# A two-layer decoder step: the VectorE order of the cached-page loop, its buffers, and two TensorE products rearranged

## The chip, the cores and the metric

The kernel runs on one core of a Trainium2 chip. TensorE (PE) multiplies matrices out of on-chip memory (SBUF) into eight accumulation banks (PSUM), VectorE (DVE) and ScalarE (ACT) read and write both, GpSimd (POOL) works on SBUF, and SyncE (SP) issues the transfers. Each engine runs its own instruction list in order and waits on semaphores. The metric is the device time of one execution in microseconds.

## What is computed

One inference step of a decoder of two layers, on a prompt of 1024 tokens and on eight samples of eight new tokens each. The three mixers of a layer are a latent attention (MLA, 8 heads), a gated linear attention and an attention over a memory. The change touches the sampled part of MLA alone: each sample attends to 32 cached pages of 128 positions, found through a page table. The core of the reference for one page:

```python
c_blk = cache_ckv[layer, phys]              # (8, 128, 256) latent
kpe_blk = cache_kpe[layer, phys]            # (8, 128, 32)  positional key, not yet rotated
k = _mla_keys(c_blk, kpe_blk, pos, w_uk, g_k)   # k_nope = c @ w_uk; rmsnorm over (k_nope, kpe); rotate the last 32
sc = einsum('bthd,bphd->bhtp', q, k) * MLA_SCALE
m_new = maximum(m, s.max(-1)); alpha = exp(m - m_new); p = exp(s - m_new[..., None])
l_new = l * alpha + p.sum(-1)
acc_new = acc * alpha[..., None] + einsum('bhtp,bpr->bhtr', p, c_blk)
```

## The kernel before

Each layer has three stages: nine tiles of projections (eight of the prompt, one of the sample), the **page loop**, and the output projection. The page loop is what changes. It takes the 8 x 32 pages of a layer in 32 groups of G = 8 pages, four groups for each sample, so 64 groups in all; `k` counts groups in a layer, `j` pages in a group, and `n0` or `np_` groups or pages over both layers. On the groups with low numbers ride small steps of the sample's other work (`sample_step(k, j)`), such as the eight products over the new tokens (`NEW_VALUES`, page steps (1,6), (1,7), (2,0) to (2,4) and (3,0)), each of which TensorE may begin when VectorE has copied out the one before.

One group, engine by engine:

- **SP** copies raw pages to a scratch tensor in DRAM in an arrangement that is cheap to transpose (`copy_pages`, L403; most are copied during the prompt, the last 28 of a layer one in each group), loads that arrangement for half a group (`load_quarters`, L420), the positional keys page by page (`load_kpe`, L412), and the pages as they are (`load_pages`, L428, which waits until the values of two groups before have been used). At the head of each group's transfers it waits until all copies issued so far have landed (`gathered`).
- **VectorE** turns the quarters into latents by position with a stream transpose (`turn_quarters`, L1017, four in a group, two pages each; `pcT_ready` tells TensorE). A ring of six such pairs lies in `region`, `xT` and `W`.
- **TensorE** multiplies each page with `w_uk` (`keys`, L1911, two products of 128x512 float32, each of which is two records in the trace), into bank 2 or 3 by turns.
- **ScalarE** squares the product (L874) into one of two buffers `sqb`, **VectorE** sums the squares for each head (L1396) into `pst`. ScalarE waits for the sum of the page two before, TensorE for the square of the page two before (`pkn_sq`).
- **GpSimd** rotates the positional keys of the eight pages (L652 to L655) and squares the unrotated ones (L656). TensorE turns the rotated ones (`rotT`, L1968) after page 1.
- After page 7 VectorE and ScalarE form the factor of each key from the sums (L1401 to L1407), while TensorE makes the scores (`scores_of`, L1927 for the latent part, L1929 for the rotary part) and then the values of the group before (`values`, L1941). VectorE scales the scores into `psb` (L1413) and takes maxima over the pages (L1415).
- The maxima of group k - 1 are finished in group k: TensorE turns them after page 3 (`maxima_T`, L1946), VectorE reduces them and lays the running maximum on a diagonal `dg` (L1424 to L1429), TensorE spreads it over all partitions with a product against ones after page 5 (`maxima_over`, L1950), VectorE subtracts (L1432) and ScalarE takes the exponential (L886).

Everything is in one hand-written order on each engine: a late instruction of VectorE holds back all of its later ones. In the rows, an instruction's names are those of the whole allocation: `w_in` holds `sqb`, `pst`, `dg`, `pm` and from group 20 on the loaded pages; `region` holds `psb`, `rotT` and the rings; `U` holds the queries.

## Time and profile before

| | |
|---|---|
| median of three runs | 2888.56 us (2888.01 to 2888.64) |
| profiled execution | 2889.7 us, of which the span from first to last instruction is 2887.9 us |
| PE busy | 2804.5 us, 97% |
| DVE busy | 1892.6 us, 66% |
| ACT busy | 880.6 us, 30% |
| POOL busy | 332.9 us, 12% |
| mean granted TensorE clock | 0.994 |

The page loops run from 664.8 to 1341.2 us and from 2078.7 to about 2757 us of the span, nearly half of it. The matmul records' ends are modelled: a record lasts about 0.16 us longer than until the next one starts, so a gap on TensorE is longer by that than the idle time that the profile prints, and gaps below 0.16 us are not printed at all.

### The profile page before, as it was taken

How to read it: one execution, taken by the hardware profiler on the slowest of the kernel's cores; microseconds unless marked ns; L12 is line 12 of the kernel's file. 1: busy time of each engine (PE TensorE's matmuls, PEld its weight loads, DVE VectorE, ACT ScalarE, POOL GpSimd, SP SyncE). 2: the span in 40 equal slices, each digit the busy share in tenths (PEclk: the TensorE clock that was granted, in tenths of full speed). 3: DMA queues.
4: the chain of work that ended last, by engine and by line, in shares of the span. 5: the costliest groups of instructions: out<-in, count | busy, mean ns of one | idle time of the engine just before them, and what ended most of it. 6: DMA issues, size and time to landing. Idle time of an engine off the chain costs nothing.

```text
span 2887.9 us, 56735 instructions
## 1 busy us (share of the span) xinstructions
PE 2804.5 (97%) x19061; PEld 1666.9 (58%) x19061; DVE 1892.6 (66%) x3801; ACT 880.6 (30%) x1903; POOL 332.9 (12%) x467
## 2 busy tenths in 40 slices
PE   8999999998999999999999999999989999999999
PEld 5666677664445554545466667767544555554553
DVE  3666665557787778776245666655678787877742
ACT  1333333432323333332023333333223333333300
POOL 1111000002111111110010000000111111111100
PEclk9999999999999999999999999999999999999999
DMA  7222223334334434543532222233443444445432
GB/s 279 73 65 68 70 72 74 72 90 137 107 108 116 124 112 124 151 147 123 212 122 59 65 69 70 71 74 72 135 113 101 115 117 123 116 121 174 116 106 84
DMA packets 528949, 313.85 MB, mean 109 GB/s; under 512 B 360009, under 2 KB 512146, under 8 KB 525586
## 3 DMA queue, kind: packets, MB, share of 16 engines
q1 hardware_dynamic: 526912, 309.41, 37.4%
q8 instruction: 152, 2.49, 0.4%
q14 instruction: 139, 1.14, 0.1%
q10 hardware_dynamic: 1746, 0.81, 0.1%
HBM read 287.63 MB, written 89.60 MB: 131 GB/s over the span
## 4 chain that ended last, share of the span: by engine, by line
PE 56%; DVE 21%; SPq 10%; DMA 6%; issue 4%; ACT 4%; POOL 0%; DVEq 0%; ACTq 0%
PE ps L1505 11%; PE ps L1911 10%; PE ps L1989 8%; DVE w_in L1396 5%; SPq L398 3%; PE ps L1739 3%; PE ps L1499 3%; PE ps L1927 3%; DMA pages_by_quarter<-in_cache_ckv 2%; SPq L428 2%; PE ps L1941 2%; DVE region L1017 2%; SPq L403 2%; PE ps L1511 2%; PE ps L1516 2%
## 5 line engine op out<-in xcount | busy, mean ns | idle before, releaser
L1911 PE MATMUL ps<-w_uk,region 128*128 128x512 f32 x1040 | 474.1, 598 | 2.9 <-ACT w_in L874 1.6
L874 ACT ACTIVATE w_in<-ps 128x512 f32<-128x512 f32 x512 | 305.7, 597 | 497.1 <-PE ps L1911 402.5
L1396 DVE TENSOR_REDUCE w_in<-w_in 128x8 f32<-128x512 f32 x512 | 351.3, 686 | 136.5 <-ACT w_in L874 121.5
L1505 PE MATMUL ps<-w_in,xT 128*128 128x256 f32 (+6 forms) x1360 | 379.1, 432 | 0.6
L1911 PE MATMUL ps<-w_uk,xT 128*128 128x512 f32 x672 | 309.0, 602 | 3.1 <-ACT w_in L874 3.1
L1911 PEld LDWEIGHTS ps<-w_uk,region 128*128 128x128 f32 x1040 | 186.3, 190 | 217.1 <-issue 206.1
L1505 PEld LDWEIGHTS ps<-w_in,xT 128*128 128x128 f32 (+1 forms) x1360 | 246.9, 186 | 111.9 <-issue 69.3
L603 POOL TENSOR_TENSOR rs<-us,mhalf 128x1 f32<-128x1 f32 (+4 forms) x132 | 130.9, 991 | 1351.1 <-DVE us L1033 729.8
L1911 PEld LDWEIGHTS ps<-w_uk,xT 128*128 128x128 f32 x672 | 121.6, 192 | 138.9 <-issue 133.8
L1911 PE MATMUL ps<-w_uk,W 128*128 128x512 f32 x336 | 151.7, 593 | 0.0
L1929 PE MATMUL ps<-U,region 128*64 128x64 f32 x2048 | 149.3, 224 | 0.0
L1739 PE MATMUL ps<-region,W 96*128 96x512 f32 (+3 forms) x384 | 147.5, 497 | 0.1
L1511 PE MATMUL ps<-w_in,xT 128*128 128x256 f32 (+1 forms) x496 | 142.9, 431 | 0.0
L1224 DVE TENSOR_REDUCE st<-ps 128x1 f32<-128x256 f32 (+7 forms) x128 | 97.0, 758 | 68.0 <-PE ps L1740 64.3
L652 POOL TENSOR_TENSOR xt<-region,mkv 128x128 f32<-128x128 f32 x64 | 29.2, 457 | 967.3 <-issue 942.0
L792 ACT ACTIVATE U<-ps,us 128x256 f32<-128x256 f32 (+7 forms) x128 | 94.8, 740 | 121.4 <-DVE us L1225 85.9
L1989 PE MATMUL ps<-region,glw 128*128 128x512 f32 x256 | 113.2, 595 | 0.0
L1989 PE MATMUL ps<-region,xT 128*128 128x512 f32 x256 | 112.3, 594 | 0.0
L1927 PEld LDWEIGHTS ps<-U,region 128*64 128x64 f32 x2080 | 86.0, 142 | 41.7 <-issue 41.7
L1927 PE MATMUL ps<-U,region 128*64 128x64 f32 x2080 | 99.9, 228 | 9.7 <-DVE U L1286 9.7
L1929 PEld LDWEIGHTS ps<-U,region 128*64 128x64 f32 x2048 | 106.2, 140 | 0.0
L1511 PEld LDWEIGHTS ps<-w_in,xT 128*128 128x128 f32 x496 | 89.4, 190 | 28.8
(403 smaller groups left out, 4183.8 us busy)
## 6 DMA issues: line engine op xcount, KB each, us to landing
pages_by_quarter<-in_cache_ckv SPq DMA_DIRECT2D x512, 128.0 KB
region<-pages_by_quarter SPq DMA_DIRECT2D x80, 512.0 KB, 4.0
region<-in_cache_ckv SPq DMA_DIRECT2D x320, 128.0 KB, 2.2
w_in<-pages_by_quarter SPq DMA_DIRECT2D x48, 512.0 KB, 4.0
w_in<-in_cache_ckv SPq DMA_DIRECT2D x192, 128.0 KB, 2.2
w_in<-in_w_in SPq DMA_DIRECT2D x16, 1240.0 KB, 10.5
mix_quarters<-xn SPq DMA_DIRECT2D x16, 512.0 KB, 3.8
region<-in_cache_kpe SPq DMA_DIRECT2D x512, 16.0 KB
```

The source lines that it names most:

```text
L603: pool.tensor_tensor(rs[0:T, c:c + k], us[0:T, c:c + k], mhalf[0:T, 0:k], ALU.pow).then_inc(s.root_ready, 1)
L792: tell(act.activation(pt[:, h % 2, 0:nk], src, ACT.Exp, bias=us[:, 52 + h % 2:53 + h % 2], scale=SCALE, accum_out=st[:, 52 + h:53 + h]), s ...
L874: tell(act.activation(sqb[:, j % 2, :], ps[:, j if k == 0 and j < 2 else 2 + j % 2, :], ACT.Square), s.pkn_sq, np_)
L1224: own(dve.tensor_reduce(st[:, 62 + h % 2:63 + h % 2], src, X, ALU.max))
L1396: tell(dve.tensor_reduce(pst[:, 0, j * H:j * H + H], heads(sqb[:, j % 2, :], H), X, ALU.add), s.pkn_red, np_)
L1505: ins = mm(out, xT[:, k, 0:T], w_in[:, k, c0:c0 + w], start=k == 0, stop=k == KD - 1)
L1511: ins = mm(out, xT[:, k, 0:T], w_in[:, k, c0:c0 + w], start=k == 0, stop=k == KD - 1)
L1739: ins = mm(ps[:, bank + c // 512, 0:w], qT[:, h, :], kT[:, h, c:c + w], start=True, stop=not last)
L1911: ins = mm(ps[:, key_bank(k, j), :], page[:, o_:o_ + P], w_uk[:, c, :], start=c == 0, stop=c == 1)
L1927: ins = mm(so, page[:, o_:o_ + 64], qt[:, c, 64 * b:64 * b + 64], start=c == 0, stop=False)
L1929: ins = mm(so, rotT[:, j // 4, half:half + 64], qrz[:, j % 4, 64 * b:64 * b + 64], start=False, stop=True)
L1989: ins = mm(ps[:, 2 + c, :], m_T[p][:, k, :], w_out[:, k, 512 * c:512 * c + 512], start=k == 0, stop=k == KD - 1)
```

## The change

The computed result is the same. Seven things move:

1. **VectorE order.** The quarters 2 and 3 of a group are turned together ahead of page 0 (before: ahead of pages 1 and 3). Quarter 0 of the next group is turned after page 5 (before: ahead of it), quarter 1 after the statistics have been handed to ScalarE (before: ahead of page 7). The reduction of the maxima moves from behind page 3 to ahead of page 2's sum (`group_max`), the subtraction from behind page 5 to behind page 4 (`less_max`), the sum of the positional squares from page 0 to page 2.
2. **Four square buffers** `sqb` in place of two. ScalarE waits for the sum of the page four before. It takes the exponential behind page 6 (before: 5).
3. **Rotary products in pairs.** In place of two products of 128 rows x 64 columns x 64 for each page (16 in a group, three quarters of whose rows meet zeros), there are eight of 64 rows x 64 columns x 128, each for two pages, after all the latent products. GpSimd writes the rotated keys in the order that this needs; it makes the squares first and rotates in place.
4. **Banks.** The scores of pages 0 to 3 go to bank 0 and those of pages 4 to 7 to bank 1 (before: all to bank 4).
5. **The product that spreads the maxima** is made as two products of 64 output partitions (`halves`).
6. **SP order.** The page copy goes ahead of the second half of the positional keys, the load of `w_out` parts ahead of them all; before, both were last.
7. **Group 1's first quarters** are loaded right behind group 0's pages, ahead of its positional keys and of the 4 MB of memory keys and values.

```diff
-        sqb = scratch[:, 16640:17664].rearrange("p (b n) -> p b n", b=2)
+        sqb = [scratch[:, o_:o_ + 512] for o_ in (16640, 17152, 18648, 19160)]
...
                 load_pages(0, held[0])
+                load_quarters(1, 0)
                 load_kpe(1, 0, G, held[1])
...
-                    load_quarters(k, 0)
+                    if k > 1:
+                        load_quarters(k, 0)
+                    if LATE + 4 <= k < LATE + 4 + NG:
...
                     load_quarters(k, 1)
+                    if copied < DB * PAGES:
+                        copy_pages(copied, copied + 1)
+                        copied += 1
                     if k + 1 < DB * NG:
                         load_kpe(k + 1, G // 2, G, held[k + 1])
                     load_pages(k, held[k])
-                    if copied < DB * PAGES:
-                        copy_pages(copied, copied + 1)
-                        copied += 1
...
-                    own(pool.tensor_tensor(kr, kp, cosp[:, tab, :], ALU.mult))
-                    own(pool.tensor_tensor(kr, kr, rt, ALU.add))
-                    pool.tensor_tensor(rtmp[:, 1, :], kpr[:, q, :], kpr[:, q, :], ALU.mult).then_inc(s.kpe_rot, 1)
+                    own(pool.tensor_tensor(rtmp[:, 1, :], kpr[:, q, :], kpr[:, q, :], ALU.mult))
+                    own(pool.tensor_tensor(kp, kp, cosp[:, tab, :], ALU.mult))
+                    pool.tensor_tensor(krot[:, q, :].rearrange("p (c r n) -> p c r n", c=2, r=2), by_half[0], by_half[1], ALU.add).then_inc(s.kpe_rot, 1)
...
-                        if np_ >= 2:
-
-                            act.wait_ge(s.pkn_red, np_ - 1)
+                        if np_ >= 4:
+
+                            act.wait_ge(s.pkn_red, np_ - 3)
...
-                    if j == 5:
+                    if j == 6:
                         act.wait_ge(s.psub_ready, n0 + 1)
...
-                        if j in (1, 3):
-                            turn_quarters(k, (j + 3) // 2)
-                        if j in (5, 7) and k + 1 < DB * NG:
-                            turn_quarters(k + 1, (j - 5) // 2)
+                        if j == 0:
+                            turn_quarters(k, 2)
+                            turn_quarters(k, 3)
                         sample_step(k, j)
...
+                        if k and j == 2:
+                            group_max(k - 1)
+                        if j == (2 if k else 3):
...
+                        if k and j == 4:
+                            less_max(k - 1)
+                        if j == 5 and k + 1 < DB * NG:
+                            turn_quarters(k + 1, 0)
...
                     tell(ts(pst[:, 1, :], pst[:, 0, :], 1.0 / QK, EPS, ALU.mult, ALU.add), s.pu_ready, n0)
+                    if k + 1 < DB * NG:
+                        turn_quarters(k + 1, 1)
                     dve.wait_ge(s.r_exp, n0 + 1)
...
+                        page, so_ = pcT(k * (G // 2) + j // 2), 64 * (j % 4)
+                        for c in range(2):
                             for half in range(0, P, 64):
...
+                                mm(ps[half:half + 64, j // 4, so_:so_ + 64], page[:, o_:o_ + 64], qt[:, c, 64 * b:64 * b + 64], start=c == 0 and j % 4 == 0, stop=False)
+                    for c in range(2):
+                        for half in range(0, P, 64):
+                            for r in range(2):
+                                w = slice(64 * r, 64 * r + 64)
+                                ins = mm(ps[half:half + 64, r, P * c:P * c + P], rotT[w, c, half:half + 64], qrz[w, 2 * r:2 * r + 2, 64 * b:64 * b + 64], start=False, stop=c == 1)
                     ins.then_inc(s.ps_ps, 1)
...
-                    mm(ps[:, 7, 384:512], ones[:], dg, start=True, stop=True).then_inc(s.pmb_ps, 1)
+                    halves(ps[:, 7, 384:512], ones[:], dg, P, True, True).then_inc(s.pmb_ps, 1)
```

**VectorE, a group with no sample steps, from the first page's sum on, before.** L1396 is a page's sum, L1017 a transpose (of two pages), L1424 to L1429 the maxima of the group before.

```order
L1396 TENSOR_REDUCE w_in<-w_in 128x8 [waits pkn_sq,kk_ready]
L1017 STREAM_TRANSPOSE region<-w_in 128x2x4x64 [waits ps_ps,bulk_in_3,pkn_red]
L1396 TENSOR_REDUCE w_in<-w_in 128x8 [waits pkn_sq,pcT_ready]
L1396 TENSOR_REDUCE w_in<-w_in 128x8 [waits pkn_sq,pkn_red]
L1017 STREAM_TRANSPOSE xT<-w_in 128x2x4x64 [waits ps_ps,bulk_in_3,pkn_red]
L1396 TENSOR_REDUCE w_in<-w_in 128x8 [waits pkn_sq,pcT_ready]
L1424 TENSOR_REDUCE w_in<-ps 128x1 [waits pmT_ps,pkn_red]
L1426 TENSOR_TENSOR w_in<-w_in,m 128x1 [waits dve_step]
L1427 TENSOR_TENSOR w_in<-m,w_in 128x1 [waits dve_step]
L1428 TENSOR_SCALAR m<-w_in 128x1 [waits dve_step]
L1429 TENSOR_SCALAR w_in<-ident,w_in 128x128 [waits dve_step]
```

The same place now; the transpose is L1018, the maxima L1427 to L1432, the sum of the positional squares L1394.

```order
L1018 STREAM_TRANSPOSE region<-w_in 128x2x4x64 [waits ps_ps,bulk_in_3,pacc_ready]
L1018 STREAM_TRANSPOSE xT<-w_in 128x2x4x64 [waits ps_ps,bulk_in_3,pcT_ready]
L1396 TENSOR_REDUCE w_in<-w_in 128x8 [waits pkn_sq,pcT_ready]
L1396 TENSOR_REDUCE w_in<-w_in 128x8 [waits pkn_sq,pkn_red]
L1427 TENSOR_REDUCE w_in<-ps 128x1 [waits pmT_ps,pkn_red]
L1429 TENSOR_TENSOR w_in<-w_in,m 128x1 [waits dve_step]
L1430 TENSOR_TENSOR w_in<-m,w_in 128x1 [waits dve_step]
L1431 TENSOR_SCALAR m<-w_in 128x1 [waits dve_step]
L1432 TENSOR_SCALAR w_in<-ident,w_in 128x128 [waits dve_step]
L1394 TENSOR_REDUCE w_in<-xt 128x8 [waits kpe_rot,pd_ready]
L1396 TENSOR_REDUCE w_in<-w_in 128x8 [waits pkn_sq,kk_ready]
```

Two page sums and the positional sum now stand behind the maxima; the transposes stand first.

**TensorE, from the last product of page 5 to the scores, before.** L1950 spreads the maxima, L1927 and L1929 are the latent and the rotary part of the scores.

```order
L1911 MATMUL ps<-w_uk,region 128x512
L1950 MATMUL ps<-w_in,ones 128x128 [waits pd_ready]
L1911 MATMUL ps<-w_uk,xT 128x512 [waits pkn_sq,pcT_ready]
L1911 MATMUL ps<-w_uk,xT 128x512
L1911 MATMUL ps<-w_uk,xT 128x512 [waits pkn_sq,pcT_ready]
L1911 MATMUL ps<-w_uk,xT 128x512
L1927 MATMUL ps<-U,region 64x64 [waits rotT_evac]
L1927 MATMUL ps<-U,region 64x64 x3
L1929 MATMUL ps<-U,region 64x64 x2
L1927 MATMUL ps<-U,region 64x64 x4
L1929 MATMUL ps<-U,region 64x64 x2
```

The same place now; L1506 is the spread in halves, L1918 the keys, L1932 and L1937 the scores, L1949 the values.

```order
L1918 MATMUL ps<-w_uk,region 128x512
L1506 MATMUL ps<-w_in,ones 64x128 [waits pd_ready]
L1506 MATMUL ps<-w_in,ones 64x128
L1918 MATMUL ps<-w_uk,xT 128x512 [waits pkn_sq,pcT_ready]
L1918 MATMUL ps<-w_uk,xT 128x512
L1918 MATMUL ps<-w_uk,xT 128x512 [waits pkn_sq,pcT_ready]
L1918 MATMUL ps<-w_uk,xT 128x512
L1932 MATMUL ps<-U,region 64x64 [waits rotT_evac]
L1932 MATMUL ps<-U,region 64x64 x23
L1932 MATMUL ps<-U,xT 64x64 x8
L1937 MATMUL ps<-U,region 64x128 x8
L1949 MATMUL ps<-region 64x257 [waits pacc_ready,bulk_in_1,pp_ready]
```

The rotary products are one block of eight between latent products and values.

**SP, at the turn of a group, before.** The copy (L403) and the load of `w_out` are followed at once by the quarters of the next group, which wait for the copy.

```order
L398 ISA x2
L403 ISA
L403 DMA pages_by_quarter<-in_cache_ckv 512x1x64
L522 DMA region<-in_w_out 128x2048
L420 DMA w_in<-pages_by_quarter 128x4x256 [waits pcT_ready,gathered]
L398 ISA x2
L412 ISA
```

Where the copy stands now, between the second quarters and the positional keys:

```order
L420 DMA w_in<-pages_by_quarter 128x4x256 [waits pcT_ready]
L398 ISA x2
L403 ISA
L403 DMA pages_by_quarter<-in_cache_ckv 512x1x64
L398 ISA x2
L412 ISA
L412 DMA region<-in_cache_kpe 128x32
```

Four positional keys and eight pages now stand between a copy and the next wait for it.

## Rows read from the trace of the kernel before

**Rows 1.** The page: engines, busy us, share, instructions.

```profile
PE 2804.5 (97%) x19061; PEld 1666.9 (58%) x19061; DVE 1892.6 (66%) x3801; ACT 880.6 (30%) x1903; POOL 332.9 (12%) x467
```

**Rows 2.** Waits of TensorE: us in total, times, longest.

```profile
PE ps L1950 <- DVE w_in L1429: 24.8, 34, 1.1
PE ps L1927 <- DVE U L1286: 9.7, 2, 4.9
...
PE ps L1911 <- ACT w_in L874: 4.6, 4, 1.6
```

**Rows 3.** Windows: length, busy of the engines, clock, DMA. Groups 20-29, group 21.

```profile
1101.38:1302.87 201.49, 195.15 (x1492) 102.34 (x1490) 157.60 (x285) 65.37 (x132) 30.09 (x50) 1.00 0.48 140
1122.37:1141.54 19.17, 19.17 (x151) 10.31 (x149) 14.58 (x26) 6.08 (x12) 2.99 (x5) 1.00 0.44 124
```

**Rows 4.** Timeline of VectorE in group 24, which starts at 1181.35.

```profile
1192.42 0.29 DVE L1424 TENSOR_REDUCE w_in<-ps 128x1 f32<-128x128 f32 x1
...
1193.33 0.29 DVE L1429 TENSOR_SCALAR w_in<-ident,w_in 128x128 f32<-128x128 f32 x1
...
1195.37 1.11 DVE L1017 STREAM_TRANSPOSE xT<-w_in 128x512 f32<-128x512 f32 x1 [1.03 <-DMA w_in<-pages_by_quarter]
...
1197.23 0.69 DVE L1432 TENSOR_TENSOR region<-region,ps 128x512 f32<-128x512 f32 x1
1199.61 0.69 DVE L1396 TENSOR_REDUCE w_in<-w_in 128x8 f32<-128x512 f32 x1 [1.69 <-ACT w_in L874]
```

**Rows 5.** SyncE: quarters issued in group 24 (timeline), and its longest wait.

```profile
1189.97 0.39 SPq L420 DMA_DIRECT2D w_in<-pages_by_quarter  x1
...
1195.40 0.43 SPq L420 DMA_DIRECT2D w_in<-pages_by_quarter  x1
...
SPq L420 <- DMA pages_by_quarter<-in_cache_ckv: 149.2, 53, 3.9
```

**Rows 6.** Timeline of TensorE in a group that waits for nothing.

```profile
1119.83 0.40 PE L1927 MATMUL ps<-U,W 128*64 128x64 f32 x8
...
1120.06 0.29 PE L1929 MATMUL ps<-U,region 128*64 128x64 f32 x4
...
1120.18 0.40 PE L1927 MATMUL ps<-U,W 128*64 128x64 f32 x8
...
1120.53 1.91 PE L1941 MATMUL ps<-region 128*64 128x257 f32 x16
...
1122.37 3.70 PE L1911 MATMUL ps<-w_uk,region 128*128 128x512 f32 x8
...
1133.11 0.38 PE L1950 MATMUL ps<-w_in,ones 128*128 128x128 f32 x2
...
1133.33 3.60 PE L1911 MATMUL ps<-w_uk,xT 128*128 128x512 f32 x8
...
1136.86 0.45 PE L1927 MATMUL ps<-U,region 128*64 128x64 f32 x8
```

**Rows 7.** Timeline of TensorE: products in two row tiles, in four column tiles.

```profile
1485.04 1.13 PE L1639 MATMUL ps<-mkv,ws 64*128 64x256 f32 x8 [0.19 <-DVE ws L1045]
...
1038.94 1.97 PE L1874 MATMUL ps<-w_in 128*32 128x256 f32 x32
```

**Rows 8.** Group 0: timelines of SyncE, VectorE, TensorE, and a window as in 3.

```profile
674.49 2.86 SPq L420 DMA_DIRECT2D region<-pages_by_quarter  x1
...
685.10 1.07 DVE L1017 STREAM_TRANSPOSE xT<-region 128x512 f32<-128x512 f32 x1 [5.06 <-DMA region<-pages_by_quarter]
...
688.88 0.70 PE L1927 MATMUL ps<-U,region 128*64 128x64 f32 x8 [4.82 <-DVE U L1286]
...
686.90:693.70 6.80, 4.83 (x91) 4.86 (x92) 6.01 (x9) 0.60 (x1) 0.00 (x0) 0.50 0.51 153
```

**Rows 9.** Timeline of TensorE in group 2, which starts at 721.70.

```profile
726.81 0.65 PE L1838 MATMUL ps<-ck,w_in 64*64 64x257 f32 x2 [0.42 <-DVE ws L1314]
...
732.47 0.65 PE L1838 MATMUL ps<-ck,w_in 64*64 64x257 f32 x2 [0.51 <-DVE ws L1314]
```

More of the change, by code:

```diff
@@ L642, in _ @@
                     rt = rtmp[:, 0, :].rearrange("p (j n) -> p j n", j=G)
-                    kr = krot[:, q, :].rearrange("p (j n) -> p j n", j=G)
+                    by_half = [x_.rearrange("p (r c n) -> p c r n", r=2, c=2) for x_ in (kpr[:, q, :], rtmp[:, 0, :])]
                     tab = slice(g * G, g * G + G)
@@ L870, in act_group @@
                         act.wait_ge(s.pkn_ps, np_ + 1)
-                        if np_ >= 2:
-                            act.wait_ge(s.pkn_red, np_ - 1)
-                        tell(act.activation(sqb[:, j % 2, :], ps[:, j if k == 0 and j < 2 else 2 + j % 2, :], ACT.Square), s.pkn_sq, np_)
+                        if np_ >= 4:
+                            act.wait_ge(s.pkn_red, np_ - 3)
+                        tell(act.activation(sqb[j % 4], ps[:, j if k == 0 and j < 2 else 2 + j % 2, :], ACT.Square), s.pkn_sq, np_)
                         if k:
@@ L889, in _ @@
                     act_group(k)
[L890 removed]
+                softmax(DB * NG - 1, 6)
                 act.wait_ge(s.fold_ready, 4 * L + 2)
@@ L1395, in dve_group @@
                         dve.wait_ge(s.pkn_sq, np_ + 1)
-                        tell(dve.tensor_reduce(pst[:, 0, j * H:j * H + H], heads(sqb[:, j % 2, :], H), X, ALU.add), s.pkn_red, np_)
-                        if k:
-                            softmax(k - 1, j)
+                        tell(dve.tensor_reduce(pst[:, 0, j * H:j * H + H], heads(sqb[j % 4], H), X, ALU.add), s.pkn_red, np_)
+                        if k and j == 4:
+                            less_max(k - 1)
+                        if j == 5 and k + 1 < DB * NG:
+                            turn_quarters(k + 1, 0)
+                        if k == DB * NG - 1 and j == G - 2:
+                            turned(0)
                     u3 = pst[:, 0, :].rearrange("p (j h) -> p j h", j=G)
@@ L1434, in gather, with less_max @@
+                def less_max(k):
+                    n0 = L * DB * NG + k
+                    sg = psb[:, k % 2, :].rearrange("p (j n) -> p j n", n=P)
+                    dve.wait_ge(s.pmb_ps, n0 + 1)
+                    tell(tt(sg, sg, over_heads(ps[:, 7, 384:512], P, G // 2, P), ALU.subtract), s.psub_ready, n0)
                 def gather(k):
@@ L1920, in scores_of @@
                     for j in range(G):
[L1921 to L1922 removed]
+                        page, so_ = pcT(k * (G // 2) + j // 2), 64 * (j % 4)
+                        for c in range(2):
                             for half in range(0, P, 64):
[L1924 to L1929 removed]
+                                o_ = (j % 2) * R + c * P + half
+                                mm(ps[half:half + 64, j // 4, so_:so_ + 64], page[:, o_:o_ + 64], qt[:, c, 64 * b:64 * b + 64], start=c == 0 and j % 4 == 0, stop=False)
[4 more added lines that the diff above has]
+                                ins = mm(ps[half:half + 64, r, P * c:P * c + P], rotT[w, c, half:half + 64], qrz[w, 2 * r:2 * r + 2, 64 * b:64 * b + 64], start=False, stop=c == 1)
                     ins.then_inc(s.ps_ps, 1)
```

47 lines of the change are left out of this document (15 added, 32 removed).

## The prediction

> **What bounds the kernel now.** I read the page first, then the waits of TensorE, then windows of whole groups, then the timelines of single groups. The page shows TensorE busy for 97% of the span and VectorE for 66% [rows 1], so time can only come from TensorE's own work or from its gaps, and only in the page loops, since nothing else is touched. The waits put the gaps of the loops at two places: the product that spreads the maxima waits 34 times for VectorE's diagonal, 24.8 us, and the first scores of each layer wait 4.8 us for the queries, 9.7 us; four key products add 4.6 us [rows 2]. A group that waits for nothing takes 19.17 us; groups 20 to 29 take 201.49 us, 9.8 us more than ten such groups [rows 3]. VectorE works 14.6 to 15.8 us of each, so it has room; it is late by its order and by what it waits for.
>
> Why it is late shows in group 24, which starts at 1181.35 and takes 20.85 us. The maxima are reduced at 1192.42 and the diagonal is ready at 1193.6, that is at 12.3; TensorE has done six pages (six times 1.72 us, and 0.33 us of turning) at 10.65. Then VectorE waits 1.03 us for a transfer, its subtraction comes at 1197.23, ScalarE sits in the exponential that needs it, and the page's square behind that exponential keeps VectorE waiting 1.69 us [rows 4]. The lateness is carried into the next group. The transfer is late because SyncE issues the quarters only when the page copy just issued has landed, a wait that sums to 149.2 us over 53 times; in group 24 they go out at 8.6 and 14.05 after the group's start [rows 5].
>
> **Part by part.** T is a group's start.
>
> *VectorE order, buffers, SyncE order (1, 2, 6).* With four square buffers neither ScalarE nor TensorE needs a recent sum, and I lay VectorE's work out with the durations of [rows 4]: a transpose 1.11, a sum or a subtraction 0.69, the maxima 1.20. The statistics of page 7 are in at about T + 15.7, the transpose of quarter 1 fills the time in which ScalarE makes the roots, the scores are scaled and the next maxima taken by T + 19.9, 0.7 into the next group. There: accumulate 1.2, two transposes 3.4, two sums 4.9, then a wait for TensorE's turned maxima, which come after page 3 at 7.4. The diagonal is ready at 8.6, 2.0 us before TensorE asks at 10.65. VectorE has 2.5 us of waiting there, which absorbs lateness instead of passing it on. SyncE no longer waits for a copy it has just issued: pages out by T + 4, quarters at 4.4 and 8.5, needed at 12.4 and at 1.2 of the next group, so some 4 us after issue there are 4 and 8 us to spare. The gain: 24.8 us; each of the 34 gaps is 0.16 us longer than printed, since the last of eight key records is printed beyond its turn (3.60 us for eight that follow each other by 0.43) [rows 6], which adds 5.5; the four key waits with theirs, 5.3; behind a gap the second record of a product starts about 0.10 late, some 40 times, 4; and short gaps ahead of page 4 that fall below what is printed, 3. That makes 43. Ten groups give 9.8 [rows 3], 64 at that rate 63, with the sample steps' own work in it; 43 lies below that. I take 41 and 25 to 43 as bounds.
>
> *First quarters (7).* In group 0 VectorE waits 5.06 us for the quarters of group 1, issued at 674.49 behind 4 MB of other loads; the query copies stand behind that transpose, TensorE waits 4.82 us for them, and then the granted clock is 0.50 of full, 1.2 instead of 2.4 GHz, for 6.8 us with 4.83 us of work in it [rows 8]. Loaded ahead of those, the quarters are there by 675. VectorE would copy the queries by 683.7, TensorE has its last key product out at 683.9. So 9.7 us over both layers go, and half of the 4.83 us that ran at half clock, some 2.1 per layer beyond the printed tails, 4.3. A second stretch of half clock follows in group 1 under products of eight columns; I leave it in. Sum 14.0, bounds 9 and 17.
>
> *Rotary products (3, 4).* A page's scores take 0.35 us, of which the rotary part is the 0.12 from 1120.06 to 1120.18 [rows 6]: 0.93 for a group. Now there are 16 records of 128 columns. 256 columns take 0.216 a wave: two row tiles of L1639 make four waves in its 1.13 us, four column tiles of L1874 eight waves in 1.97 [rows 7]. So 128 columns take 0.109, and four quadrants at once make 4 waves, 0.44. No row has row and column tiles together. Changing between tile shapes costs: eight key records should end at 1133.33 + 8 x 0.429 = 1136.76, the scores start at 1136.86, 0.10 later; 16 values records should end at 1120.53 + 8 x 0.216 = 1122.26, the keys start at 1122.37, 0.11 later, and the first keys then take 3.70 instead of 3.60 [rows 6]. The block adds two changes, each 0.10 and about 0.04 for the first wave's weights: 0.27. Net 0.93 - 0.44 - 0.27 = 0.22, 64 times: 14 gained. Bounds: all four never at once, 8 waves, 14 lost; changes free, 31 gained.
>
> The Trainium skill, page "TensorE: Matmul & The Clock Gate", section "Measured speedup vs the span model", has row and column tiles running together, 16 of them at 10.6 times. By it the 4 waves hold and the sum stays; the other reading is a rival below.
>
> *The spread in halves (5).* Before: 0.22 us from 1133.11 to 1133.33, no change of shape. Now two waves of 128 columns, the same 0.22, and a change in and out in the middle of the keys: 0.10 and 0.04 in, 0.11 out and 0.10 on the first keys [rows 6]. 0.34, 64 times: 22 lost. Bound below: where TensorE still waited, the way in is free, 0.2 each, 13.
>
> The Trainium skill speaks against this part: page "TensorEngine Tiling (Array Packing)", section "Key Properties", says that changing the tiling mode drains TensorE. The 0.10 of the rows agrees. The page gives no price; by a reading with free changes the result would be 22 us better and the rotary part 17.
>
> *New waits.* Two transposes now stand ahead of the sample steps of page 0, and the maxima ahead of those of pages 2 and 3. In group 2, TensorE's products over the new tokens each need VectorE's copy of the last. At page 1 the copy comes at about T + 4.1 where TensorE asks at 1.9; at page 4 it comes behind the maxima, at 14.3 where TensorE asks at 11.5. 5.0 against the 0.9 waited there now [rows 9], 4.1 for each layer, 8; in group 1 ScalarE's square waits for the sample's scores, 1 for each layer. Together 10, bounds 2 and 14. GpSimd's reordering, the banks and the earlier `w_out` cost nothing: keys are rotated by T + 12 for the next group's page 1, and quarters have 4 us to spare.
>
> *Sum.* -41 - 14 - 14 + 22 + 10 = -37. From the profiled execution's own 2889.7 us: 2852; it lies 1.1 us above the median of the runs, so **2851**.
>
> **Rivals.** *Quadrants go two at a time.* The pairs of records start alternately, and nothing shows four with half the rows each. For it: no row. Against it: both kinds of tile run side by side singly [rows 7]. 8 waves, 28 us more: 2879.
>
> *The stalls only move.* VectorE now stands still at the maxima until TensorE turns them. If its chain from page 7 is 2 us or more longer than laid out, it comes there late and the diagonal is late as before; half of the 41 stays: 2872. Against it: VectorE's sum of work is 15 of 19 us [rows 3].
>
> *Cheaper switches and a full clock.* If changes cost half and the second low-clock stretch also goes: 2835.
>
> *Slower: the second quarters late.* Two transposes stand at the head of each group's VectorE work, and the second of each two halves must have landed by T + 1.2. If it lands after about T + 4, the diagonal is late, and everything behind: each further us is paid in every group, 62 times. It decides where SyncE issues them: at 8.5 of the group before they are there; at 14.05 or later, as now [rows 5], with 4 us for landing, they are just there. At 1 us a group, 2851 + 62 = 2913; from 0.6 us a group on the change is slower.
>
> *The change does little.* If waits and switches cancel, within 6 us of 2889.
>
> **How the numbers follow.** The forecast with 2838 to 2866 gets 0.60, cheaper switches 0.14, two at a time 0.12, stalls that move 0.08, slower 0.04, little 0.02. The range 2829 to 2877 takes the forecast, the cheaper switches and the moved stalls, and leaves out the rest. Within 0.2% (5.8 us) is about what a measurement of this kernel can't tell from no change: faster 0.94, same 0.02, slower 0.04.
>
> **What would show it.** The wait at the spread gone from TensorE's waits, and groups 20 to 29 at 19.2 to 19.3 us each, near 193 in all, says that the order works; above 196, that stalls moved. The eight rotary products in 0.44 us and not 0.9. The key products behind the spread 0.2 late. The first scores near 684 with the clock at 1.00. Waits of the new-token products up from 0.9 to 5 us in group 2. SyncE's wait for copies near nothing. The prediction is wrong if a queue that I call idle enough, SyncE's above all, is not.

## The result and the profile after

| | before | changed |
|---|---|---|
| median | 2888.28 us (2887.35 to 2888.64, 4 runs) | 2853.16 us (2848.47 to 2855.34, 4 runs) |
| profiled execution: span | 2887.9 us | 2850.6 us |
| PE busy | 2804.5 us | 2799.9 us |

The ratio is 0.9877 (95% interval 0.986 to 0.9894): 35 us less. The forecast was 2851 us, the range 2829 to 2877. The page of the changed kernel, first line as in [rows 1]:

```profile
PE 2799.9 (98%) x18165; PEld 1634.6 (57%) x18165; DVE 1890.1 (66%) x3801; ACT 881.2 (31%) x1903; POOL 329.8 (12%) x467
```

TensorE's work has hardly shrunk; the span has lost what it stood still. The waits of TensorE, longest in total first (us, times, longest), are to be read against [rows 2]:

```profile
PE ps L1845 <- DVE ws L1315: 11.0, 4, 3.0
PE ps L1529 <- DVE xn L941: 8.3, 1, 8.3
...
PE ps L1845 <- DVE w_in L1311: 3.2, 2, 1.6
```

Neither the spread (now L1506) nor the first scores nor a key product waits any more, and the page copies no longer stand among what SyncE waits for. In their place stand four waits of the products on the new tokens for VectorE's copy (L1845 behind L1315), two in group 2 of each layer; before, the same four summed to 1.9 us. The two waits behind L1311, in group 1, were there before (3.1 us). Windows (length; busy us of PE, PEld, DVE, ACT, POOL; clock; DMA share; GB/s) of group 0, group 2 of the first layer, groups 20 to 29, and group 2 of the second layer:

```profile
664.36:689.00 24.64, 24.48 (x219) 15.05 (x217) 22.76 (x41) 7.84 (x14) 7.84 (x12) 1.00 0.70 210
713.99:747.22 33.23, 27.74 (x147) 12.06 (x146) 18.70 (x37) 6.50 (x13) 2.97 (x5) 0.85 0.25 73
1092.14:1285.43 193.29, 193.29 (x1353) 97.78 (x1351) 157.45 (x284) 64.97 (x130) 29.81 (x50) 1.00 0.49 144
...
2112.63:2142.95 30.32, 24.82 (x147) 11.16 (x146) 18.71 (x37) 6.50 (x13) 2.97 (x5) 0.94 0.27 79
```

Group 0 took 31.9 us and has lost 7. Groups 20 to 29 took 201.49 us [rows 3] and now take 193.29: ten equal groups of 19.33 us, TensorE busy throughout. That is 0.16 more than the 19.17 of a group that waited for nothing before, so the two rearranged products together cost time, and the waits have given more than the whole gain. Group 2 is the loss: 33.2 and 30.3 us where 23.9 stood, TensorE idle for 5.5 us and then at a granted clock of 0.50 for some stretches, which gives the mean of 0.85 and 0.94.

A group's time is read from its first key product to that of the next. Summed over both layers, in us:

| groups | 0 | 1 | 2 | 3 to 8 | 9 to 19 | 20 to 30 |
|---|---|---|---|---|---|---|
| before | 63.5 | 49.9 | 47.8 | 268.0 | 443.4 | 444.1 |
| changed | 49.3 | 50.0 | 63.5 | 249.5 | 440.4 | 425.3 |
| e9, old VectorE order | 49.4 | 50.2 | 48.1 | 275.4 | 440.4 | 425.8 |
| e10, new order alone | 62.4 | 48.8 | 59.9 | 250.3 | 437.0 | 424.2 |
| e12, the fastest | 49.6 | 49.4 | 47.2 | 244.0 | 429.5 | 413.4 |

The columns of the changed kernel differ from those of before by 38.7 us; 1.4 us come back outside them. Groups 0, 1 and 2 also differ between executions of one kernel, by where the clock falls to half.

How VectorE now goes through group 24 (it starts at 1169.46), as [rows 4] did for before:

```profile
1177.03 0.29 DVE L1427 TENSOR_REDUCE w_in<-ps 128x1 f32<-128x128 f32 x1 [1.77 <-PE ps L1954]
...
1177.93 0.29 DVE L1432 TENSOR_SCALAR w_in<-ident,w_in 128x128 f32<-128x128 f32 x1
...
1180.87 0.69 DVE L1439 TENSOR_TENSOR region<-region,ps 128x512 f32<-128x512 f32 x1
...
1185.14 0.69 DVE L1396 TENSOR_REDUCE w_in<-w_in 128x8 f32<-128x512 f32 x1 [1.00 <-ACT w_in L875]
```

It stands still for 1.77 us until TensorE has turned the maxima, has the diagonal ready at 8.8 us of the group (8.6 was laid out, 12.3 stood before), and TensorE asks at 10.8. The statistics of page 7 are in at 16.4 (15.7 was laid out), and the next maxima are taken 1.5 us into the next group (0.7 was laid out).

TensorE in the same group, from the keys of pages 4 and 5 over the spread to the rotary block and the values (against [rows 6]):

```profile
1176.76 3.60 PE L1918 MATMUL ps<-w_uk,region 128*128 128x512 f32 x8
...
1180.29 0.44 PE L1506 MATMUL ps<-w_in,ones 128*64 128x128 f32 x4
...
1180.66 3.70 PE L1918 MATMUL ps<-w_uk,xT 128*128 128x512 f32 x8
...
1186.30 0.67 PE L1937 MATMUL ps<-U,region 64*64 64x128 f32 x16
...
1186.90 1.96 PE L1949 MATMUL ps<-w_in,region 128*64 128x257 f32 x16
```

The spread starts 0.10 after the keys should have ended (1176.76 + 3.43), lasts 0.37 to the next keys where the whole product lasted 0.22, and those keys take 3.70 instead of 3.60. The sixteen rotary records stand in 0.60 us, way out included. Two at a time they would need eight waves of 0.109 us, 0.87. In the single records of the trace four start within 0.02 us, the next four 0.16 us after the first, then four each 0.11 us later: four go at once.

### The profile page after: what moved, and what is told of

It reads as the page before. It is cut to its first block, busy times and chain, and to the rows that moved or that the text cites. A ratio compares the mean times of both kernels' runs of the same rounds, so it can differ in the third digit from the quotient of the medians.

```text
span 2850.6 us, 54943 instructions
## 1 busy us (share of the span) xinstructions
PE 2799.9 (98%) x18165; PEld 1634.6 (57%) x18165; DVE 1890.1 (66%) x3801; ACT 881.2 (31%) x1903; POOL 329.8 (12%) x467
## 4 chain that ended last, share of the span: by engine, by line
PE 86%; DVE 7%; SPq 3%; ACT 2%; issue 1%; DMA 0%; POOL 0%; DVEq 0%; ACTq 0%
PE ps L1918 31%; PE ps L1512 12%; PE ps L1997 8%; PE ps L1932 4%; PE ps L1949 4%; PE ps L1506 4%; PE ps L1746 3%; PE ps L1711 2%; PE ps L1518 2%; PE ps L1523 2%; PE ps L1771 2%; PE ps L1937 1%; SPq L398 1%; SPq L403 1%; ACT U L730 1%
## 5 line engine op out<-in xcount | busy, mean ns | idle before, releaser
L1918 PE MATMUL ps<-w_uk,region 128*128 128x512 f32 x1040 | 475.0, 599 | 0.0
L1396 DVE TENSOR_REDUCE w_in<-w_in 128x8 f32<-128x512 f32 x512 | 351.3, 686 | 90.2 <-ACT w_in L875 74.9
L1918 PE MATMUL ps<-w_uk,xT 128*128 128x512 f32 x672 | 313.6, 611 | 0.0
L1918 PEld LDWEIGHTS ps<-w_uk,region 128*128 128x128 f32 x1040 | 186.8, 190 | 214.2 <-issue 213.5
L1918 PEld LDWEIGHTS ps<-w_uk,xT 128*128 128x128 f32 x672 | 123.5, 194 | 140.1 <-issue 139.8
L1918 PE MATMUL ps<-w_uk,W 128*128 128x512 f32 x336 | 153.7, 599 | 0.0
L1238 DVE COPY ws<-ps 128x512 f32<-128x512 f32 (+3 forms) x64 | 37.9, 592 | 99.6 <-PE ps L1771 98.7
L1918 PEld LDWEIGHTS ps<-w_uk,W 128*128 128x128 f32 x336 | 60.3, 190 | 62.9 <-issue 62.7
L1771 PE MATMUL ps<-ident,U 128*128 128x128 f32 x576 | 89.2, 282 | 7.0 <-ACT U L793 6.3
L1018 DVE STREAM_TRANSPOSE region<-region 128x512 f32<-128x512 f32 x82 | 90.9, 1109 | 5.2 <-DMA region<-pages_by_quarter 2.3
```

Source lines behind the costliest of these rows:

```text
L1396: tell(dve.tensor_reduce(pst[:, 0, j * H:j * H + H], heads(sqb[j % 4], H), X, ALU.add), s.pkn_red, np_)
L1771: ins = tp(ps[:, b, (j % 4) * P:(j % 4) * P + P], pt[:, h % 2, j * P:j * P + P], ident[:])
L1918: ins = mm(ps[:, key_bank(k, j), :], page[:, o_:o_ + P], w_uk[:, c, :], start=c == 0, stop=c == 1)
```

## The experiments

Twelve kernels ran, each compared with the kernel before on the same chip (medians of before 2886.64 for e1 to e4, 2887.65 for e5 to e8, 2888.32 for e9 to e12). The changed kernel's four runs belong to a set of their own (before: 2888.28), so differences to it cross sets and are uncertain by a few us; the times of groups agree more closely. e4, e5 and e12 build on each other; the others start from the kernel that their row names.

| | kernel | median, us | ratio to before (95%) |
|---|---|---|---|
| | changed | 2853.16 | 0.9877 (0.986 to 0.9894) |
| e1 | changed, spread whole | 2827.5 | 0.9793 (0.978 to 0.9807) |
| e2 | changed, rotary single | 2859.32 | 0.9906 (0.9891 to 0.9921) |
| e3 | changed, sample steps first | 2833.47 | 0.9814 (0.98 to 0.9827) |
| e4 | e1 and e3 | 2814.3 | 0.9751 (0.9737 to 0.9764) |
| e5 | e4, rotary block first | 2804.37 | 0.9706 (0.9692 to 0.972) |
| e6 | before, early quarters | 2872.98 | 0.9946 (0.9931 to 0.9962) |
| e7 | changed, old SyncE order | 2849.74 | 0.9871 (0.9854 to 0.9888) |
| e8 | changed, two buffers | 2855.61 | 0.9887 (0.987 to 0.9904) |
| e9 | changed, old VectorE order | 2866.31 | 0.9923 (0.9908 to 0.9937) |
| e10 | before, new VectorE order | 2854.39 | 0.9881 (0.9865 to 0.9896) |
| e11 | before, spread in halves | 2903.3 | 1.005 (1.0035 to 1.0065) |
| e12 | e5, rotated keys turned first | 2800.82 | 0.9696 (0.9683 to 0.9709) |

### e10 and e9: is it the order?

e10 puts the change's VectorE order, and ScalarE's exponential behind page 6, into the kernel before, and nothing else. "The order" below means both; they were not separated.

> The kernel before with VectorE's new order alone (and the exponential behind page 6): two buffers, SyncE's old order, late first quarters, single rotary products, whole spread. Theory A, the order alone removes the waits: 41 less, group 2's 16 more, 2888 - 25 = 2863 us, plain groups at 19.17. Theory B, it needs the buffers or SyncE's order too: 2880 or more, plain groups with waits at the spread.

Measured 2854.39 us, 34 less: as much as the whole change. Windows of groups 20 to 29 and of group 2, and the only printed waits of TensorE in groups 3 to 30:

```profile
1095.34:1288.44 193.10, 191.97 (x1492) 103.13 (x1490) 157.25 (x284) 64.95 (x130) 29.79 (x50) 1.00 0.50 146
...
721.70:751.67 29.97, 24.67 (x160) 11.68 (x160) 18.52 (x37) 6.50 (x13) 2.97 (x5) 0.94 0.27 80
...
PE ps L1916 <- ACT w_in L874: 2.8, 8, 1.1
```

Nine of the ten groups take 19.17 us, one waits 1.3 us, for a square. Theory A holds: the order needs neither the buffers nor SyncE's new order to remove the waits at the spread. It gives 9 us more than the 25 expected: groups 3 to 30 lose 44 us and not 41, group 2 loses 12 and not 16 to the new waits, and groups 0 and 1 take 2 less. The whole change removes 49 us of waits in groups 3 to 30, so some 5 us, key products that wait for squares among them, go only with the rest of it.

e9 is the reverse: the changed kernel with VectorE's old order, and ScalarE's exponential behind page 5 again.

```diff
-                    if j == 6:
+                    if j == 5:
                         act.wait_ge(s.psub_ready, n0 + 1)
...
-                        if j == 0:
-                            turn_quarters(k, 2)
-                            turn_quarters(k, 3)
+                        if j in (1, 3):
+                            turn_quarters(k, (j + 3) // 2)
+                        if j in (5, 7) and k + 1 < DB * NG:
+                            turn_quarters(k + 1, (j - 5) // 2)
...
-                        if k and j == 2:
-                            group_max(k - 1)
-                        if j == (2 if k else 3):
+                        if j == (0 if k else 3):
...
-                        if k and j == 4:
+                        if k and j == 3:
+                            group_max(k - 1)
+                        if k and j == 5:
                             less_max(k - 1)
-                        if j == 5 and k + 1 < DB * NG:
-                            turn_quarters(k + 1, 0)
...
-                    if k + 1 < DB * NG:
-                        turn_quarters(k + 1, 1)
```

> The changed kernel with VectorE's old order (quarters ahead of pages 1, 3, 5 and 7, the maxima behind page 3, the subtraction behind page 5, ScalarE's exponential behind page 5); four buffers, SyncE's order, early quarters, paired rotary products and the spread in halves stay. Group 2's waits of 15.7 us over both layers should go, since its copies stand first again. Theory A, the prediction's: only the order brings the diagonal in time, and 41 us of waits come back: 2878 us. Theory B: with four buffers VectorE is never held by a square behind the exponential, its lateness no longer adds up, and the diagonal is ready near 9.4 us of the group, where TensorE asks at 10.65: no waits in plain groups (19.33 us), 2853 - 16 = 2837 us.

Measured 2866.31 us, 13 more than the changed kernel: between the two theories. Its longest wait of TensorE, and the windows of groups 20 to 29 and 3 to 8:

```profile
PE ps L1503 <- DVE w_in L1429: 19.6, 11, 3.1
...
1094.96:1288.80 193.84, 193.36 (x1352) 97.77 (x1351) 157.60 (x284) 64.94 (x130) 29.83 (x50) 1.00 0.48 144
738.90:874.79 135.89, 126.81 (x856) 65.14 (x856) 111.25 (x214) 43.58 (x83) 20.10 (x31) 0.99 0.37 105
```

In the plain groups the waits stay away without the order (193.84 and not 201.49), with one wait of 0.5 us. There VectorE waited 10.1 us for transfers before and now waits for none, and ScalarE's waits for VectorE's sums fall from 24.0 to 9.0 us; the diagonal is ready at 10.2 us in nine of the ten groups, 0.6 ahead of the asking. Which part of the rest of the change does it was not tried, and Theory B's own reason is not borne out: VectorE is still held up to 1.7 us by the square behind the exponential. In groups 3 to 8, where sample steps add work to VectorE, the other ten waits of the first line stand, up to 3.1 us, some with half clock behind them, and 26 us come back; group 2, freed of its new waits, gives 15. So Theory B's forecast holds for the plain groups and Theory A's for the loaded ones: the plain waits are removed twice over, those of groups 3 to 8 by the order alone.

### e7 and e8: SyncE's order and the buffers

e7 moves the page copies and the parts of `w_out` back to the end of each group's transfers.

> The changed kernel with SyncE's copies and the parts of w_out last in a group again; the early quarters stay. SyncE then waits for the landing of each copy, about 3.5 us in groups 1 to 28, and issues quarters at 8 and 13 to 14 us of a group. Theory A, that VectorE's new order needs the second quarters at 1.5 us of the next group and they are there at 18: no change within 3 us in most groups, up to 5 us in all where parts of w_out are loaded. Theory B, that the earlier quarters are what lets the order work: plain groups of 19.33 only where nothing is copied, 20 us more or over.

Measured 2849.74 us (2848.29 to 2854.46), the changed kernel's time. SyncE's wait for the copies is all there, VectorE waits for quarters in groups 20 to 29 (the two DVE lines), and the window of these groups doesn't show it:

```profile
SPq L420 <- DMA pages_by_quarter<-in_cache_ckv: 155.0, 54, 3.6
...
DVE region L1019 <- DMA w_in<-pages_by_quarter: 8.2, 6, 3.8
DVE xT L1019 <- DMA w_in<-pages_by_quarter: 1.7, 1, 1.7
...
1088.47:1281.76 193.29, 193.29 (x1353) 97.85 (x1351) 157.25 (x284) 64.94 (x130) 29.78 (x50) 1.00 0.50 145
```

The 149.2 us of [rows 5] cost nothing in the new order. The quarters go out as late as before (9.4 and 14.8 us into group 24), and VectorE waits for them as long as before (9.9 us in these ten groups; 10.1 before). But all seven waits are for the next group's first quarters, 13 us or more into a group, behind the diagonal; what VectorE stands still there it stands still less at the next maxima (12.6 us in these groups; 16.7 in the changed kernel). Theory A holds.

e8 has `sqb[j % 2]` and ScalarE's old wait (`np_ >= 2`, `pkn_red, np_ - 1`).

> The changed kernel with two square buffers instead of four. The square of page 4 then waits for the sum of page 2, which stands behind the maxima (at about 10 us of the group, where page 4's product is done at 9.1), TensorE's page 6 starts at 11.2. Theory A, that this is covered: within 3 us of 2853. Theory B, that ScalarE's lateness reaches TensorE: key products wait for squares, 0.3 us or more in each group, 20 us more.

Measured 2855.61 us (2851.89 to 2858.22), and again 193.29 us for groups 20 to 29; groups 3 to 8 take 0.9 us more over both layers. Theory A holds: in the changed kernel the buffers are spare. What the change does without both the buffers and SyncE's order was not run; e10 lacks both. Whether buffers alone or SyncE's order alone would cure the plain groups of the kernel before was not tried.

### e6: the early quarters alone

```diff
                 load_pages(0, held[0])
+                load_quarters(1, 0)
                 load_kpe(1, 0, G, held[1])
```

> The kernel before with part 7 alone (group 1's first quarters ahead of its positional keys and of the memory loads). Theory A, that this alone removes the wait of VectorE for the transfer, of TensorE for the queries and the half clock behind it: 14 us less (9 to 17), 2873 us, group 0 at 24.6 us instead of 31.9. Theory B, that it needs VectorE's new order too: under 5 us.

Measured 2872.98 us, 15 less. Group 0 falls to 24.8 us, at full clock:

```profile
662.44:687.26 24.82, 24.66 (x235) 15.48 (x233) 22.58 (x40) 7.62 (x14) 7.84 (x12) 1.00 0.76 223
```

The waits of the other groups stay (202.44 us for groups 20 to 29). Theory A holds.

### e1 and e11: the spread in halves

e1 undoes part 5 in the changed kernel.

```diff
-                    halves(ps[:, 7, 384:512], ones[:], dg, P, True, True).then_inc(s.pmb_ps, 1)
+                    mm(ps[:, 7, 384:512], ones[:], dg, start=True, stop=True).then_inc(s.pmb_ps, 1)
```

> The changed kernel with the spread of the maxima as one product of 128x128 again, nothing else. Theory A, that the halves only cost changes of tile shape: in the changed kernel's trace the key product ahead of them is followed 0.09 us late, the two waves with the way out take 0.37 us where one whole product takes 0.22, and the next key's second record comes 0.10 late, 0.345 us in all, 64 times: 22 us less, 2831 us, and groups without sample steps at 18.98 us instead of 19.33. Theory B, that the halves bring the spread out sooner and something behind needs that: the same time or more, 2853 or above, with VectorE's subtraction or the exponential late.

Measured 2827.5 us, 26 less. Groups 20 to 29:

```profile
1084.97:1274.82 189.85, 189.85 (x1333) 98.85 (x1331) 157.37 (x284) 64.95 (x130) 29.79 (x50) 1.00 0.49 147
```

18.98 us a group, 0.344 less: 22 of the 26 us. The rest has no one place. In the profiled executions, 24.9 us apart, the half clock fell otherwise: group 2 takes 3.7 us less over both layers, group 1 takes 2.1 more, and about 4 us less lie outside the columns of the table, where the kernels are all but the same. Theory A holds. e11 puts the halves into the kernel before:

> The kernel before with the spread in halves alone. Where TensorE doesn't wait there, 0.345 us more in a group; where it does (34 printed waits, some 40 in all), the way in is hidden and the whole product's late second record (0.10) goes: 0.2 less the 0.10, about 0.1 to 0.2 more. Theory A: 24 x 0.345 + 40 x 0.15 = 14 us more, 2902 us. Theory B, that the halves help where the diagonal is late (a reason to have them): 2888 or less.

Measured 2903.3 us, 15 more. A group of that kernel in which TensorE waits for the diagonal:

```profile
1217.97 0.44 PE L1499 MATMUL ps<-w_in,ones 128*64 128x128 f32 x4 [0.82 <-DVE w_in L1429]
1218.34 3.70 PE L1911 MATMUL ps<-w_uk,region 128*128 128x512 f32 x8
```

The way in hides in the wait, the way out doesn't: the spread still takes 0.37, the keys behind it 3.70. Theory A holds (14 expected).

### e2 and e5: the rotary block

e2 makes the rotary part page by page again, on the keys as they now lie.

```diff
...
-                    for c in range(2):
...
-                            for r in range(2):
-                                w = slice(64 * r, 64 * r + 64)
-                                ins = mm(ps[half:half + 64, r, P * c:P * c + P], rotT[w, c, half:half + 64], qrz[w, 2 * r:2 * r + 2, 64 * b:64 * b + 64], start=False, stop=c == 1)
+                            ins = mm(ps[half:half + 64, j // 4, so_:so_ + 64], rotT[:, j % 4 // 2, half:half + 64],
+                                     qrz[:, 2 * (j // 4) + j % 2, 64 * b:64 * b + 64], start=False, stop=True)
```

> The changed kernel with one rotary product for each page and half again (128 rows, 64 columns, between the latent products), on the rotated keys as they now lie. Theory A, four quadrants at once and two more changes of shape: the block with its changes costs 0.75 us in the changed kernel, the single products 0.93, so 0.19 us more in each of 64 groups: 12 us more, 2865 us, plain groups at 19.52 us. Theory B, that the pairing brings nothing once its changes are paid: 2853 within 2.

Measured 2859.32 us, 6 more. Groups 20 to 29:

```profile
1091.80:1286.96 195.16, 195.16 (x1512) 102.04 (x1510) 157.27 (x284) 64.95 (x130) 29.82 (x50) 1.00 0.47 143
```

19.52 us a group, 0.19 more as expected, 12 in all; group 2, with a shorter time at half clock, gave 3 of them back, and the runs of the changed kernel spread over 7 us. Theory A holds in size for the group; half of it shows in the median.

e5 puts the rotary block ahead of the latent products, on top of e4:

```diff
+                    for c in range(2):
+                        for half in range(0, P, 64):
+                            for r in range(2):
+                                w = slice(64 * r, 64 * r + 64)
+                                mm(ps[half:half + 64, r, P * c:P * c + P], rotT[w, c, half:half + 64],
+                                   qrz[w, 2 * r:2 * r + 2, 64 * b:64 * b + 64], start=c == 0, stop=False)
```

(The latent products follow with `start=False, stop=c == 1 and j % 4 == 3`; the block that stood behind them is taken out.)

> The kernel of e4 with the rotary block ahead of the latent products. The way into the 64-row tiles then falls on the change that the keys' end pays anyway, and the values follow the latent products without one: one change of shape less in each group. Theory A, a change costs 0.10 us and 0.04 for the first wave: 64 times 0.14, 9 us less than e4's 2814, 2805 us, plain groups at 18.84 us instead of 18.98. Theory B, that small weights loaded right behind the wide key products start later: same as e4.

Measured 2804.37 us, 10 less than e4. TensorE from the last keys to the next:

```profile
1162.43 0.67 PE L1931 MATMUL ps<-U,region 64*64 64x128 f32 x16
1163.03 1.62 PE L1937 MATMUL ps<-U,region 128*64 128x64 f32 x48
1164.48 0.64 PE L1937 MATMUL ps<-U,xT 128*64 128x64 f32 x16
1164.95 1.91 PE L1949 MATMUL ps<-w_in,region 128*64 128x257 f32 x16
1166.79 2.41 PE L1918 MATMUL ps<-w_uk,xT 128*128 128x512 f32 x5
```

The values now take 1.91 and not 1.96: they follow products of their own shape. Groups 20 to 29 take 188.37 us, 0.15 less each. Theory A holds.

### e3 and e4: the new waits of group 2

```diff
+                        sample_step(k, j)
                         if j == 0:
                             turn_quarters(k, 2)
                             turn_quarters(k, 3)
-                        sample_step(k, j)
-                        if k and j == 2:
+                        if k and j == (3 if k == 2 else 2):
                             group_max(k - 1)
```

> The changed kernel with VectorE's sample step of page 0 ahead of the two transposes and, in group 2 alone, the maxima behind the copy of page 3. Theory A, that these two places make group 2's waits of 2.5 and 3.0 us in each layer, and the waits the stretches of half clock behind them: groups 2 fall from 33.2 and 30.3 to near 24.2 us, 15 us less, 2838 us. Theory B, that the half clock comes from the small products on new tokens themselves: only the waits go, 10 us less, 2843 us. Theory C, that turning the quarters later makes the keys wait: no gain.

Measured 2833.47 us, 20 less. In the changed kernel the two waits look so (TensorE, then VectorE's copies for them):

```profile
718.49 0.64 PE L1845 MATMUL ps<-ck,w_in 64*64 64x257 f32 x2 [2.52 <-DVE ws L1315]
...
730.93 1.11 PE L1845 MATMUL ps<-ck,w_in 64*64 64x257 f32 x2 [2.98 <-DVE ws L1315]
731.97 6.24 PE L1918 MATMUL ps<-w_uk,xT 128*128 128x512 f32 x8
...
718.02 0.42 DVE L1315 COPY ws<-ps 64x257 f32<-64x257 f32 x1
...
730.46 0.42 DVE L1315 COPY ws<-ps 64x257 f32<-64x257 f32 x1
```

Behind the second wait eight key records take 6.24 us instead of 3.60: the granted clock is 0.50 for most of them. With the steps first, group 2 takes 24.05 us at a clock of 1.00:

```profile
714.35:738.40 24.05, 23.12 (x146) 10.57 (x145) 18.71 (x37) 6.50 (x13) 2.98 (x5) 1.00 0.34 100
```

Both layers together take 48.1 us, 15.4 less, and the profiled executions differ by 15.6. Theory A holds; the median fell 5 us further than it said, which no group shows. The small products of group 2 are the same in both kernels, so the half clock does not come from them alone (Theory B). Both moves were made together; which of them removed which wait was not separated. e4 has both mends:

> Both: the spread whole and the sample steps first. If the two losses are independent, 22 + 15 = 37 us less than the changed kernel: 2816 us. If the whole spread makes VectorE's slack too small somewhere, the gain is less than the sum.

Measured 2814.3 us, 39 less than the changed kernel for 37 expected: within what these runs can tell, the losses are independent.

### e12: the rotated keys turned first

`turn_rotated` holds the wait and the two transposes that stood behind page 1.

```diff
+                        if k and j == 0:
+                            turn_rotated(k)
                         keys(k, j)
```

> The kernel of e5 (whole spread, sample steps first, rotary block first) with the rotated keys turned ahead of page 0 instead of behind page 1. Groups 9 to 16, where transposes already stand ahead of the keys after the change of shape, show no late second record (0.10 us). Theory A, that a transpose's weights, being quicker to load, take that place everywhere: 0.10 less in some 46 groups, 5 us less than e5's 2804, 2800 us, plain groups at 18.74 us. Theory B, that the late record only moves behind the transposes: same as e5.

Measured 2800.82 us, 3.5 less than e5 for 4 to 5 expected. The first transposes and keys of a group, and groups 20 to 29:

```profile
1163.34 0.44 PE L1963 MATMUL ps<-ident,xt 128*128 128x128 f32 x2
1163.62 3.60 PE L1918 MATMUL ps<-w_uk,xT 128*128 128x512 f32 x8
...
1069.67:1257.57 187.90, 187.90 (x1333) 98.08 (x1331) 156.84 (x284) 64.98 (x130) 29.79 (x50) 1.00 0.50 149
```

The keys take 3.60 and no longer 3.70, but the two transposes take 0.28 until the keys start, where 0.22 was enough behind page 1: half of the late record moves to them. A group takes 0.05 less and not 0.10, midway between the theories. Over groups 3 to 30 of both layers that is 1.8 us of the 3.5; most of the rest lies outside the page loops, where the profiled execution of e5 has three stretches of half clock ahead of the last us and that of e12 has none. The runs of the two kernels overlap (2801.33 to 2807.02 and 2799.61 to 2801.77), so the median's agreement with the 4 to 5 is partly luck. e12 has the lowest median here, 3% less than before.

## Why the prediction was right

**The total** came out 2 us from the forecast (the sum unrounded is 2851.6). That it is so near is luck: the first term was 8 us too small, the last 6 us too small the other way, and the rotary term 2 too large.

| term | predicted | measured |
|---|---|---|
| waits of groups 3 to 30 | -41 | -49 |
| first quarters, group 0 | -14 | -14 (e6: -15) |
| rotary pairs | -14 | -12 by the groups of e2, -6 by its median |
| spread in halves | +22 | +22 by the groups of e1, +26 by its median |
| new waits, groups 1 and 2 | +10 | +16 |
| whole | -37 | -37 as the sum of the terms by groups; -35 by the medians |

**Waits.** Groups 3 to 30 lost 40.3 us although the two products cost 0.155 more in each of the 56 groups, 8.7 us: so 49 us of waits went. The term was sized from printed waits and their hidden tails and lay 8 us low, and 49 is outside its bounds of 25 to 43. The laid-out times hold up to the diagonal (0.2 us late in group 24) and less behind it: the statistics of page 7 come 0.7 and the next maxima 0.8 us later than laid out, which VectorE's standing still at the maxima takes up (1.77 us are left of the 2.5). What doesn't hold is a part of the reason: the prediction counted SyncE's earlier quarters and the four buffers among the causes and gave the 149 us of SyncE's wait a place in the chain. e7 and e8 show that in the changed kernel each alone is worth nothing or 1 us, and e10 that without both the order still removes 44 of the 49 us; e9 shows that the plain groups lose their waits without the order as well.

**Rotary pairs.** The four quadrants go at once, so the rival of two at a time is out; the block takes 0.60 us, not 0.44 + 0.14, and the values behind it 1.96, not 1.91, which makes 0.19 a group for 0.22. The 0.04 for the first wave's weights had no row behind it; the single records show the second wave 0.05 late. **The halves** cost 0.344 us a group where 0.34 stood.

**New waits.** Both were placed and sized: 2.5 and 3.0 us for 2.2 and 2.8. Left out was what the chip does after them: the clock granted is half for one or two stretches, and a key record then takes 0.85 us instead of 0.43. Group 2 lost 15.7 us over both layers for 8: some 9 by the waits (5.5 us for 0.9 in each layer), the rest by the clock. Group 1 lost nothing of its 2. The prediction had priced half clock behind the old wait of group 0 and not behind the new ones. Group 2 is also where a kernel differs from itself (33.2 us in one layer, 30.3 in the other of the same execution). But the waits don't explain how far the runs of a kernel lie apart: e3, without them, spreads over 8.1 us, e10, with them, over 1.9, and the kernel before over 1.3 in one set and over 10 in another.

**The rivals.** Stalls that only move: VectorE waited 1.8 us at the maxima in group 24 and absorbed there what it was late. Slower by late second quarters: e7 issues them as late as before, VectorE never waits for them in groups 20 to 29 and nothing is lost, so the margin that the rival turned on was there. Cheaper switches and a full clock: a change of shape cost what was read, or 0.05 us more, and the half clock of group 1 stayed. This rival's 2835 isn't worked out in the prediction; halving the changes alone makes 20 us (0.135 and 0.17 in 64 groups), 2831.

## What to carry to other kernels

Put what another engine waits for early in an in-order list, and the engine's own standing still right ahead of it; but look up what rides on the same list in the few loaded iterations, where the same move made the only new loss. A product that changes the tile shape between others of one shape pays about 0.2 us on the way back into wide products: group the narrow ones, start with the narrowest where the shape changes anyway, and don't split one that is whole. Parts that come in one change can each seem needed: taking the parts out showed two of them (the buffers, SyncE's order) to be idle, each by itself, and one (the halves) to cost 22 to 26 us where the whole change gained 35. The banks, GpSimd's new order and ScalarE's later exponential had no run of their own.

## What the runs showed of the hardware

- Sixteen float32 records of 64 rows x 64 columns x 128 take 0.60 us with the way out, in 64x64 tiles four at a time, as the two kinds of tile do singly [rows 7].
- The price of a tile shape has two parts: the next record starts 0.09 to 0.10 us late, and the second of the first wide records another 0.10 (3.70 for 3.60), or half of that where transposes stand first (e12). The identity of a transpose loads in 141 ns and the weights of a key product in 190 (the weight loads of group 24), which would fit; that it is the reason is not shown. A wait hides the way in alone (e11).
- Waits of TensorE were followed by 1.2 GHz instead of 2.4 (a granted clock of 0.50): in group 0 before, behind 4.8 and 4.9 us, and in group 2 of the six kernels with the new waits (changed, e1, e2, e7, e8, e10), where each layer has one or two such stretches behind two waits of 2.3 to 3.0 us. Not every one of these waits is followed by one: in the changed kernel's second layer only that of 3.0 us is. In the eight other kernels group 2 has none. The two waits, 5.5 us together, thus cost 6.4 to 9.3 us (30.3 and 33.2 for 23.9). In group 1 of the changed kernel the clock also falls to 0.50, at 689.3 us, behind products of eight columns and with no wait.
